# Feed-forward products scaled after the gemm instead of before it, in a two-layer hybrid decoder step

## What is computed

```python
h = rms_norm(x, g_mix_pre);  proj = h @ w_in           # conv inputs, q, k, v, gates
o = retention(q, k, v, state)                           # 4 heads, state per sequence
y_ret = (silu(g_ret) * layer_norm(o)) @ w_ret_out
z = depthwise_conv31(concat(old rows, ca * sigmoid(cb)))
merged = sigmoid(ga) * y_ret + sigmoid(gb) * (silu(layer_norm(z)) @ w_conv_out)
x = x + rms_norm(merged @ w_o, g_mix_post)
h2 = rms_norm(x, g_ffn_pre)
f = (silu(h2 @ w_ffn_gate) * (h2 @ w_ffn_up)) @ w_ffn_down
x = x + rms_norm(f, g_ffn_post)
```

## Time and profile before

| | |
|---|---|
| median of 3 runs | 1566.42 us (1566.14 to 1571.51) |
| the profiled execution | 1567.79 us |
| its span on the core | 1566.0 us |
| PE busy | 1513.0 us, 97% |
| DVE busy | 1107.8 us, 71% |
| ACT busy | 674.4 us, 43% |
| POOL busy | 287.5 us, 18% |
| mean granted TensorE clock | 0.993 of full |

### The profile page before, as it was taken

How to read it: one execution, slowest core, us unless ns; L and a number is a source line. 1 busy time by engine, 2 the same in 40 slices (tenths; PEclk the granted TensorE clock), 3 DMA queues, 4 the chain that set the end, 5 groups by cost and what they waited for, 6 DMA issues and landing times.

```text
span 1566.0 us, 25591 instructions
## 1 busy us (share of the span) xinstructions
PE 1513.0 (97%) x9840; PEld 1399.5 (89%) x9840; DVE 1107.8 (71%) x1735; ACT 674.4 (43%) x993; POOL 287.5 (18%) x257
## 2 busy tenths in 40 slices
PE   6999999999999999999999999999999999999997
PEld 5997878687999999999999978788789998999997
DVE  6699978977757567654456988989685665655544
ACT  4333434355355354334343334344464544443433
POOL 6974000011110029910000400101002000000000
PEclk9999999999999999999999999999999999999999
DMA  6554755647444434444444555658554342544443
GB/s 255 175 193 158 275 201 216 229 175 256 135 149 147 157 110 146 157 148 158 156 152 158 195 207 216 245 183 311 180 184 161 135 148 68 175 148 148 155 156 117
DMA packets 64540, 275.48 MB, mean 176 GB/s; under 512 B 7232, under 2 KB 7232, under 8 KB 55232
## 3 DMA queue, kind: packets, MB, share of 16 engines
q1 hardware_dynamic: 52560, 192.17, 35.8%
q0 software_dynamic: 11888, 82.04, 13.9%
HBM read 230.30 MB, written 43.89 MB: 175 GB/s over the span
## 4 chain that ended last, share of the span: by engine, by line
PE 79%; DVE 14%; ACT 3%; issue 1%; POOL 1%; DVEq 0%; ACTq 0%
PE bank L415 23%; PE bank L417 22%; PE bank L416 22%; DVE acc L1060 4%; DVE wlo L1025 3%; PE bank L602 2%; DVE state L1091 1%; PE bank L580 1%; DVE tmp L1080 1%; PE bank L563 1%; PE bank L516 1%; DVE x L1376 1%; ACT L770 1%; DVE tmp L1374 1%; PE bank L545 1%
## 5 line engine op out<-in xcount | busy, mean ns | idle before, releaser
L415 PE MATMUL bank<-hhi,whi 128*128 128x320 f32 x2016 | 654.5, 325 | 1.6 <-DVE wlo L1025 1.6
L417 PE MATMUL bank<-hhi,wlo 128*128 128x320 f32 x2016 | 625.2, 310 | 0.0
L416 PE MATMUL bank<-hlo,whi 128*128 128x320 f32 x2016 | 624.8, 310 | 0.0
L1025 DVE TENSOR_TENSOR wlo<-wring,whi 128x1024 fp32r<-128x1024 f32 x363 | 470.4, 1297 | 217.0 <-ACT whi L763 194.5
L415 PEld LDWEIGHTS bank<-hhi,whi 128*128 128x128 f32 x2016 | 380.8, 189 | 33.6 <-issue 29.3
L416 PEld LDWEIGHTS bank<-hlo,whi 128*128 128x128 f32 x2016 | 381.1, 189 | 8.6 <-issue 7.7
L763 ACT ACTIVATE whi<-wring 128x1024 fp32r<-128x1024 f32 x264 | 278.1, 1055 | 241.4 <-PE bank L417 239.1
L417 PEld LDWEIGHTS bank<-hhi,wlo 128*128 128x128 f32 x2016 | 380.5, 189 | 0.0
L1060 DVE SCALAR_TENSOR_TENSOR acc<-up,par,acc 128x256 f32<-128x256 f32 x480 | 211.1, 507 | 0.2
L789 ACT ACTIVATE whi<-wring 128x1024 fp32r<-128x1024 f32 x96 | 101.2, 1054 | 73.3 <-PE bank L417 72.0
L793 ACT ACTIVATE sig<-bank 128x320 f32<-128x320 f32 x92 | 40.2, 437 | 199.6 <-PE bank L417 187.2
(11 more groups left out here) (157 smaller groups left out, 1948.1 us busy)
## 6 DMA issues: line engine op xcount, KB each, us to landing
wring<-w SPq DMA_DIRECT2D x364, 512.0 KB, 3.7
state<-r_in POOLq DMA_DIRECT2D x32, 1024.0 KB, 7.6
rs_out<-state POOLq DMA_DIRECT2D x32, 1024.0 KB, 5.0
rp_out<-pst POOLq DMA_DIRECT2D x8, 512.0 KB, 8.4
us<-c_in POOLq DMA_DIRECT2D x2, 1216.0 KB, 5.7
cs_out<-us POOLq DMA_DIRECT2D x2, 1216.0 KB, 9.4
cp_out<-up POOLq DMA_DIRECT2D x2, 1144.0 KB, 5.9
con<-consts POOLq DMA_DIRECT2D x1, 1420.0 KB, 9.3
```

The lines of the kernel that those rows point to most:

```text
L415: pe.matmul(bank[g][:, 0:T], whi[j][:, k, :], hi, start=start and k == 0, stop=False)
L416: pe.matmul(bank[g][:, 0:T], whi[j][:, k, :], lo, start=False, stop=False)
L417: mm = pe.matmul(bank[g][:, 0:T], wlo[j][:, k, :], hi, start=False, stop=stop and k == n - 1)
L1025: return dve.tensor_tensor(dst, value, hi.bitcast(F32), ALU.subtract)
```

## The change

1. **The join ahead of the feed-forward.** PE no longer multiplies h2 but x times the gain alone: ACT writes the high half directly from x (Copy with the gain as its scale), DVE the low half in one instruction (`x_low`), both as soon as the tile of x is there. The two tiles of `post` become groups of 1, 1, 2, 2 and 2 tiles. The squares of x are added four to two by DVE (`add_squares`, twice), and their four matmuls lie inside `first_units`, after its sixth and seventh tile. The `stat` with its eight matmuls and 20 dummy ones goes.
2. **The feed-forward.** The scale per token is applied to the products: DVE multiplies the gate product by it out of PSUM, ACT applies Silu in place of Sigmoid, DVE multiplies the up product by the scale out of PSUM, and then the two with each other. That is three DVE instructions a pair of units instead of two.
3. **Weight splits ahead of the scale.** The split of unit 4 of the feed-forward comes before the scale of WO's norm on ACT and on DVE, the next one before (DVE) or right behind (ACT) the scale of the second norm.
4. **The start.** DVE adds the eight squares to four, PE runs 18 dummy matmuls and then four matmuls of the mean instead of eight; ACT's preload of the table set with Ln and Exp goes; POOL starts `past_taps` only when all of h is there.
5. **Orders in the heads.** In units 4 and 5 the first two state updates, and the statistics of the third token block, come ahead of DVE's weight split; the second half of the updates of quad 2 moves on PE from (4, 7) to (4, 5); the taps are spread otherwise, 8 of them now in CIN of the first layer.

The diff, with what is left out marked:

```diff
-ROPES, CONVS, POSTS = 12, TAPS, 16
+ROPES, CONVS, POSTS, POSTS0 = 12, TAPS, 18, 10
+
+MIX_GROUPS = ((0, 1), (1, 1), (2, 2), (4, 2), (6, 2))
+
 
 PAST_OPS, NEW_OPS = 2 * PAD, 2 * DS
 SAMPLE_OPS = PAST_OPS + NEW_OPS
-CIN_TAPS = (0, 2)
-FIRST_HEAD_TAPS = ((1, 2, 1, 1, 1, 2, 2, 1, 1, 1, 1, 2), (2, 2, 2, 2, 2, 2, 2, 1, 1, 1, 1, 2))
-HEAD_TAPS = ((7, 0, 3, 0, 4, 1, 5, 4, 3, 0, 0, 0), (7, 0, 3, 0, 3, 1, 4, 3, 2, 0, 0, 0))
-GB_TAPS = ((6, 0, 3, 3, 3, 1, 4, 0), (5, 0, 3, 3, 2, 1, 3, 0))
-RET_TAPS = ((1, 2, 2, 2, 0, 0), (1, 2, 2, 1, 0, 0))
+CIN_TAPS = ((1, 1, 1, 1, 2, 2), (2, 2, 2, 2, 2, 2))
+FIRST_HEAD_TAPS = ((1, 1, 1, 1, 1, 1, 1, 1, 1, 0, 0, 1), (2, 2, 2, 2, 2, 2, 2, 1, 1, 1, 1, 2))
+HEAD_TAPS = ((5, 0, 3, 0, 3, 1, 5, 3, 3, 0, 0, 0), (7, 0, 3, 0, 4, 1, 5, 4, 3, 0, 0, 0), (7, 0, 3, 0, 3, 1, 4, 3, 2, 0, 0, 0))
+GB_TAPS = ((6, 0, 3, 3, 3, 2, 4, 0), (5, 0, 3, 3, 2, 1, 3, 0))
+RET_TAPS = ((2, 2, 2, 2, 0, 0), (1, 2, 2, 1, 0, 0))
 FFN_FIRST = 3
 
 
@@ -73,7 +76,7 @@
...
-UPDATE_AT = ((1, 0), (1, 3), (1, 5), (1, 7), (4, 3), (4, 7), (5, 3), (5, 5))
+UPDATE_AT = ((1, 0), (1, 3), (1, 5), (1, 7), (4, 3), (4, 5), (5, 3), (5, 5))
...
@@ -352,6 +358,8 @@
                 if l == 0:
                     pool.wait_ge(par_loaded, 16)
                     pool.wait_ge(u_loaded, 16)
+
+                    pool.wait_ge(h_ready, KT)
                     past_taps(0, past0, stap, par[:, G_CB:G_CW], par[:, G_CW:NPAR])
...
-            def first_units(l, q, ready):
+            def first_units(l, q, ready, between=None):
 
                 pe.wait_ge(lo_done, l * UNITS + (q * RING + AHEAD))
                 for k in range(UB):
@@ -437,6 +445,8 @@
                         mm = pe.matmul(bank[j][:, 0:T], wlo[j][:, k, :], hhi[:, k, :], start=False, stop=(k == UB - 1))
                         if k == UB - 1:
                             mm.then_inc(unit_done, 1)
+                    if between is not None:
+                        between(k)
...
-                stat(l, 0, lambda k: sq8[:, k, :], KT, ones_d, lambda k: pe.wait_ge(sq_done, l * SQS + (k + 1))).then_inc(stat_done, 1)
+                if l == 0:
+                    keep_clock(18)
+                    for k in (0, 1, 4, 5):
+                        pe.wait_ge(x_halves, k // 4 + 1)
+                        mm = pe.matmul(X[:, 0:T], ones_d[:, :], sq8[:, k, :], start=(k == 0), stop=(k == 5))
+                    mm.then_inc(stat_done, 1)
+                else:
+                    stat(l, 0, lambda k: sq8[:, k, :], KT, ones_d, lambda k: pe.wait_ge(sq_done, l * SQS + (k + 1))).then_inc(stat_done, 1)
 
                 keep_clock(12)
                 first_units(l, 0, lambda k: h_read(l, k))
@@ -721,13 +738,25 @@
                          ready=(lambda k: pe.wait_ge(m_ready, l * 8 + (k + 1))) if n == 0 else None,
                          between=lambda k: square_means(l, 0, SQ_POST, n, k))
                 square_mean(l, SQ_POST, KT - 1).then_inc(stat_done, 1)
-                keep_clock(20)
-                pe.wait_ge(stat_read, l * STATS + (ST_POST + 1))
-                stat(l, 0, lambda k: sq8[:, k, :], KT, ones_d,
-                     lambda k: pe.wait_ge(sq_done, l * SQS + (SQ_FFN + k + 1))).then_inc(stat_done, 1)
-
                 keep_clock(12)
-                first_units(l, U_GU // RING, lambda k: h_read(l, 8 + k))
+
+                def half_mean(i):
+
+                    pe.wait_ge(sq_halves, l * 2 + (i + 1))
+                    if i == 0:
+                        pe.wait_ge(stat_read, l * STATS + (ST_POST + 1))
+                    for k in (4 * i, 4 * i + 1):
+                        mm = pe.matmul(X[:, 0:T], ones_d[:, :], sq8[:, k, :], start=(k == 0), stop=(k == 5))
+                    return mm
+
+                def both_halves(k):
+
+                    if k == 5:
+                        half_mean(0)
+                    if k == 6:
+                        half_mean(1).then_inc(stat_done, 1)
+
+                first_units(l, U_GU // RING, lambda k: h_read(l, 8 + k), between=both_halves)
                 unit(l, U_GU // RING, AHEAD, AHEAD, h_tile)
                 with pe.Fori(1, FT // 2) as i:
                     for j in range(4):
...
                 act.activation(sq8[:, k, :], x[:, k, :], ACT.Square).then_inc(sq_done, 1)
             act.wait_ge(memset_done, 2)
-            log_exp_table()
             def merged_half(l, n):
...
                 squares_of_products(l, U_WO, 1, SQ_POST)
+                split(l, U_GU)
                 act.wait_ge(stat_done, l * STATS + (ST_POST + 1))
                 rsqrt(l, X[:, 0:T], ST_POST, RS_POST)
-                for k in range(KT):
-                    act.wait_ge(post_step, l * POSTS + (k // 2 * 2 + 2))
-                    act.activation(sq8[:, k, :], x[:, k, :], ACT.Square).then_inc(sq_done, 1)
+                for i, (k0, n) in enumerate(MIX_GROUPS):
+                    act.wait_ge(post_step, l * POSTS + (2 * i + 2))
+                    for k in range(k0, k0 + n):
+                        act.activation(hhi[:, k, :], x[:, k, :], ACT.Copy, scale=g_(G_FFNPRE + k)).then_inc(h_hi, 1)
+                    for k in range(k0, k0 + n):
+                        act.activation(sq8[:, k, :], x[:, k, :], ACT.Square).then_inc(sq_done, 1)
                 act.wait_ge(stat_done, l * STATS + (ST_FFN + 1))
                 rsqrt(l, X[:, 0:T], ST_FFN, RS_FFN)
-                halves_of_h(l, 1)
...
+                split(l, U_GU + 1)
                 for n in range(FT):
-                    split(l, U_GU + 2 * n)
-                    if n >= 4:
-                        act.wait_ge(ffn_step, l * (2 * FT) + (2 * (n - 4) + 1))
-                    gemm(l, U_GU + 2 * n)
-                    sigmoid(sig[:, n % 4, :], bank[(2 * n) % 4][:, 0:T])
+                    if n:
+                        split(l, U_GU + 2 * n)
+                    act.wait_ge(ffn_step, l * (2 * FT) + (2 * n + 1))
+                    act.activation(sig[:, n % 4, :], sig[:, n % 4, :], ACT.Silu).then_inc(sig_done, 1)
                     if n:
                         f_half(n - 1)
-                    split(l, U_GU + 2 * n + 1)
+                    if n:
+                        split(l, U_GU + 2 * n + 1)
...
-            def updates(l, hd, j):
+            def first_updates(l, hd, j):
 
                 if j in (1, 4, 5):
                     q = (1, 4, 5).index(j)
-                    for i in range(2 if q == 0 else 0, QUAD):
-                        if j == 5 and i == 2:
-                            token_stats(l, hd, 1, range(2, 3))
-
-                            dve.wait_ge(bn_done, (l * HEADS + hd) * 3 + 3)
+                    for i in range(2):
                         update(l, hd, (0, 8, 12)[q] + i)
-                    if j == 5:
-                        token_mean_var(range(2, 3))
+                if j == 5:
+                    token_stats(l, hd, 1, range(2, 3))
+
+                    dve.wait_ge(bn_done, (l * HEADS + hd) * 3 + 3)
+                if j == 6:
+                    token_shift(l, hd, 1, slice(2, 3))
+
+            def updates(l, hd, j):
+
+                if j == 5:
+                    token_mean_var(range(2, 3))
+                if j in (1, 4, 5):
+                    q = (1, 4, 5).index(j)
+                    for i in range(2, QUAD):
+                        update(l, hd, (0, 8, 12)[q] + i)
                 if j == 1:
                     for i in range(QUAD):
                         update(l, hd, QUAD + i)
@@ -1208,13 +1249,10 @@
             def head(l, hd, first):
 
 
...
-                taps = (FIRST_HEAD_TAPS if first else HEAD_TAPS)[l]
+                taps = FIRST_HEAD_TAPS[l] if first else HEAD_TAPS[2 if l else min(hd - 1, 1)]
                 for j in range(HEAD_UNITS):
-                    if j == 1 and not first:
-                        update(l, hd - 1, 0)
-                        update(l, hd - 1, 1)
-                    if j == 6 and not first:
-                        token_shift(l, hd - 1, 1, slice(2, 3))
+                    if not first:
+                        first_updates(l, hd - 1, j)
                     split(l, U_HEAD + j, hd)
...
+            for i in range(2):
+
+                dve.wait_ge(sq_done, 4 * i + 4)
+                dve.tensor_tensor(sq8[:, 4 * i:4 * i + 2, :], sq8[:, 4 * i:4 * i + 2, :], sq8[:, 4 * i + 2:4 * i + 4, :],
+                                  ALU.add).then_inc(x_halves, 1)
...
+                    if sub == 0:
+                        split(l, U_GU)
...
+                def x_group(l, step, k, n):
+
+                    y = tmp[:, k % 4:k % 4 + n, :]
+                    scale = rstd[:, :].rearrange("p (o t) -> p o t", o=1).to_broadcast([P, n, T])
+                    dve.tensor_tensor(y, acc[:, k:k + n, :], scale, ALU.mult).then_inc(post_step, 1)
+                    dve.wait_ge(post_step, l * POSTS + (step + 1))
+                    dve.tensor_tensor(x[:, k:k + n, :], x[:, k:k + n, :], y, ALU.add).then_inc(post_step, 1)
+
+                def x_low(k):
+
```

(40 more changed lines are left out.)

45 lines of the change are left out of this document (18 added, 27 removed).

## The result

| | before, on this chip | after |
|---|---|---|
| median | 1566.68 us (4 runs) | 1554.38 us (1553.73 to 1555.67, 4 runs) |
| ratio | | 0.9916, interval 0.9895 to 0.9936 |
| profiled execution | 1567.79 us | 1553.73 us |
| its span | 1566.0 us | 1551.9 us |

The change is faster by 12.3 us, where 24.5 were foretold; 1554.38 lies 1.4 us above the range that was foretold (1531 to 1553). Of the page, PE fell by 13 us, DVE rose by 43; the mean clock is 0.993 as before.

What follows compares the result with a forecast made beforehand. PE, busy 97%, was taken to bound the kernel through waits, dummy matmuls and half clock. Terms -9.2 + 0 - 1.6 + 1.5 - 9.1 - 6.1 = -24.5 took the profiled 1567.8 to 1543.3, median 1541.9 us; range 1531 to 1553.

Steps and rivals of the forecast that it cites:

- The joins: Joins ahead of both feed-forwards: 5.1 us gained each, less 0.5 each for the clock, term -9.2.
- The heads: Heads and first layer's gate units: shorter waits for state updates -9.1, three stretches at half clock gone -6.1.
- behind 1.3 none did: Heads, (5, 5): no half-clock stretch followed 1.3 us waits, so with waits of 1.1 the three stretches go, -6.1.
- rival (b): Heads and joins: waits of 1.1 us and the joins' gaps still bring half clock, 1548 to 1553; chance 0.17.
- The feed-forward: Feed-forward loop: DVE's added product and a wait up to 0.9 fit in 7.03 us a pair; zero, bounds 0 and 3.
- if PE waits for DVE in the feed-forward loop: Feed-forward loop: one of three signs named beforehand that would show the forecast wrong.
- rival (e): Feed-forward loop becomes DVE's, over 7.03 us a pair; 0.8 us excess ends slower, at 1576; chance 0.04.
- The row: Feed-forward beside past_taps: profile row giving 0.92 us for a DVE instruction with both operands in SBUF.
- Retention output: Retention output, layer 1: no loss foretold, 0 us.
- The start: Start through first head: 8.7 us ahead at the fourth unit, most given back; -1.6, plus 1.5 for the clock.
- the reload's chain: First head: POOL's later state store and reload, landing at 161.3, let PE be at most 1 to 2 us ahead.
- DVE's full list: Convolution inputs and first head: DVE gets 17.4 us of taps, then a head with nearly no idle time.

Runs made afterwards that it cites:

- p_join: The kernel before with the joins, the feed-forward and the moved weight splits alone (parts 1 to 3): 1564.70 us, ratio 0.9978.
- p_heads: The kernel before with the orders in the heads alone, taps as before: 1553.52 us, ratio 0.9906.
- c_early: c_base without POOL's wait for h, so past_taps starts beside normalised as before the change: 1542.39 us, ratio 0.9825.
- c_cin0: c_base with layer 1's taps out of the convolution inputs, 16 in the first head and two more in the second: 1543.47 us, ratio 0.9827.
- c_rope: c_table with the rotation ahead of the taps in units 1 and 3 of the first head, both layers: 1541.51 us, ratio 0.9831.
- c_table: c_base with the table of Ln and Exp loaded first of all: 1538.30 us, ratio 0.9799.
- c_base: The changed kernel with the loop's second weight split ahead of the low half, and layer 1's gate B and retention taps as before: 1544.14 us, ratio 0.9831.

## Why the prediction was wrong

**The joins: right.** The working was 5.1 us each before the clock; 5.3 measured, in four places (both joins of the changed kernel and of p_join). The half us for the clock did not come. The path was as told: the first product 5.10 us behind the square and the fourth unit 19.3 behind it, where the working had 5.1 and 19.4; PE idles 1.13, 0.41 and 0.48 us ahead of three of the first tiles.

**The heads: right, with luck in the clock.** −15.2 foretold in both layers and the gate units, −16.9 measured. The waits foretold for (5, 5) were 0.3, 1.1 and 1.1 us, and they measure 0.33, 1.12 and 1.11; the old stretches at half clock are gone. But the reason that I gave for the last, "behind 1.3 none did", doesn't hold. `p_join` keeps the old order: there, 3.4 us at half clock follow a wait of 1.28 and none follow one of 2.07:

```profile
171.77 0.50 PE L587 MATMUL bank<-vst,kst 32*128 32x512 f32 x2 [2.07 <-DVE state L1114]
...
945.10 0.49 PE L587 MATMUL bank<-vst,kst 32*128 32x512 f32 x2 [1.28 <-DVE state L1114]
```

```profile
945.90:949.30 3.40, 3.40 (x15) 3.40 (x14) 2.72 (x8) 1.77 (x4) 1.05 (x2) 0.50 0.47 175
171.90:175.30 3.40, 3.40 (x23) 3.15 (x24) 3.25 (x8) 1.77 (x4) 0.68 (x2) 1.00 0.46 154
```

Five of the experiments with the new order have one such stretch behind the 1.1 us wait of the third head, and the changed kernel happens to have none. A part of rival (b) was right.

**The feed-forward: the step that failed.** I wrote "4.7 + 0.9 = 5.6 of 7.03, and a wait of up to 0.9 for Silu and the high half: covered, at zero", with 3 us as the bound. Two errors lie in it. First, the price: the new product did cost 0.8 to 1.1, but each other instruction of two SBUF operands grew as well. By the starts, a turn's work rose from some 4.9 us to 7.5: `flo` by 0.4, the two splits by 0.4 and 1.0, the product 0.75, the rest a few hundredths each. In the kernel before, one of the two splits came behind a wait for ACT and ran in 1.23 to 1.43 us; now it comes right behind another instruction and meets POOL, 2.31. Before:

```profile
605.62 1.23 DVE L1025 TENSOR_TENSOR wlo<-wring,whi 128x1024 fp32r<-128x1024 f32 x1 [0.79 <-ACT whi L763]
```

An average of busy time over the old order does not hold for the new one. Second, the wait was not carried into the sum: work and wait follow one another in one list. 5.6 and 0.9 would still have been covered; 7.5 and 0.9 make the 8.42. The forecast's own sign of being wrong, "if PE waits for DVE in the feed-forward loop", is what came. The rival (e), "the feed-forward loop becomes DVE's", had this mechanism, at a chance of 0.04 as a case slower than before. It put the whole turn at 7.5, half a microsecond above PE's 7.03, so that the lead would absorb the excess; 7.5 is the work alone, and at 8.2 to 8.4 the excess is 1.2 to 1.4. Its smaller form, the layer beside POOL alone, should have been a bound of the forecast: once the lead is gone, some 1 us in each of six or seven pairs.

The row decided for the smaller price, and the Trainium skill was nearer. Its page "SBUF — State Buffer", section "Who interferes with whom", says that a DVE instruction with both inputs in SBUF and a GpSimd one that reads SBUF shut each other out for their whole length; by it I had 7.0 for DVE's work in a turn (an estimate), where 7.5 was measured. The trace agrees: the same split takes 1.23 alone and up to 2.32 beside POOL, `flo` 0.49 and up to 1.39, 1.1 and 0.9 more, where POOL's two instructions take 1.06 and 1.42, while the two products that read PSUM keep 0.48 throughout.

**Retention output: a cost I did not write down, the second step that failed.** The change's tables moved a tap into a stretch whose last reader is POOL, and from there PE. I costed the taps moved to the front and not those moved to the back, so this term stood at nothing; it measured 4.3, 1.6 us more of waiting and 2.6 of clock.

**The start: nearly right for the wrong reason.** I put −1.6 + 1.5 for it all, and +1.3 came (+2.6 against the starts of p_join and p_heads, and 21.30, on which I built, is the late one of three). "Most of it is given back" holds, and more: −9.75 at the fourth unit, +1.26 at the end of the first head. But of my two reasons, the reload's chain is refuted for the first head. I had POOL free for its first state store at 148.4; it was free at 140.9 and then waited 7.51 us for DVE, PE's query at (4, 3) came at 162.32 without a wait, and in c_early the store waits 16.33 us for DVE with POOL idle. The other reason, DVE's full list, is what PE waits for; c_cin0 and c_rope show that reordering moves the debt and c_table that earlier work pays a part. The two loads were right, at 1.28 each, with the next instruction 1.29 behind the load's start.

**The clock.** Beside the start's, I costed one new stretch at half clock; there were three (94.2, 107.9 and 404.9), each at the end of a wait of over 3 us.

So the changed kernel lost 7.5 in the loop, 4.3 in retention output, 1.4 at the start and 0.4 in the second layer's convolution output beyond the sum, and won 3.1 beyond it at the joins and heads: 10.5 in all. With the first two taken out, c_base comes to −23.1.
